# A hand-scheduled two-block network on one core: the order in which VectorE's tile transposes of the gated hidden layer are placed

## The reference

```python
def swiglu(x, w13, w2):                      # w13: 1024 x 5632, w2: 2816 x 1024
    a, b = jnp.split(x @ w13, 2, axis=-1)
    return (jax.nn.silu(a) * b) @ w2
...
for l in range(DEPTH):                       # first block
    x = layer_norm(ALPHA * x + 0.5 * swiglu(x, ffn1_w13[l], ffn1_w2[l]), ...)
    m = mixer(x, ...)
    x = layer_norm(ALPHA * x + m, ...)
    x = layer_norm(ALPHA * x + 0.5 * swiglu(x, ffn2_w13[l], ffn2_w2[l]), ...)
...
for layer in range(DEPTH):                   # second block
    h = swiglu_2(rms_norm(x, g[0]), ffn_w_in[layer, 0], ffn_w_out[layer, 0])
    x = x + 0.5 * rms_norm(h, g[1])
    h = token_mixer(rms_norm(x, g[2]), ...)
    x = x + rms_norm(h, g[3])
    h = swiglu_2(rms_norm(x, g[4]), ffn_w_in[layer, 1], ffn_w_out[layer, 1])
    x = x + 0.5 * rms_norm(h, g[5])
```

## Time and profile before

| what | value |
|---|---|
| median of three runs | 2129.59 us (2129.24 to 2132.51) |
| profiled execution, its own time | 2129.24 us |
| its span, first to last instruction | 2127.5 us |
| TensorE busy, matmuls | 2107.3 us, 99%, 10584 instructions |
| VectorE busy | 1698.3 us, 80%, 3204 instructions |
| ScalarE busy | 1075.8 us, 51%, 1540 instructions |
| mean granted TensorE clock | 0.999 |
| read from HBM | 390.75 MB, 184 GB/s |

### The profile page before, as it was taken

How to read it: one execution, slowest core, us unless ns; L and a number is a source line. 1 busy time by engine, 2 the same in 40 slices (tenths; PEclk the granted TensorE clock), 3 DMA queues, 4 the chain that set the end, 5 groups by cost and what they waited for, 6 DMA issues and landing times.

```text
span 2127.5 us, 28888 instructions
## 1 busy us (share of the span) xinstructions
PE 2107.3 (99%) x10584; PEld 1775.9 (83%) x10584; DVE 1698.3 (80%) x3204; ACT 1075.8 (51%) x1540; POOL 67.9 (3%) x107
## 2 busy tenths in 40 slices
PE   8999999999999999999999999999999999999998
PEld 7888999888888899978878888878888888888887
DVE  6887766888888867688888886789889888678886
ACT  5444553544444455444454446565445445665443
POOL 0000010000000001000010000010000000001000
PEclk9999999999999999999999999999999999999999
DMA  7766754666566574656656666337666665634663
GB/s 248 239 196 180 209 181 144 214 193 197 187 201 197 168 230 146 198 182 196 196 164 218 194 189 182 125 111 222 196 189 199 200 195 168 183 129 143 196 193 102
DMA packets 313952, 393.71 MB, mean 185 GB/s; under 512 B 17828, under 2 KB 272052, under 8 KB 313812
## 3 DMA queue, kind: packets, MB, share of 16 engines
q1 hardware_dynamic: 309120, 375.52, 57.7%
q0 software_dynamic: 4528, 16.29, 2.3%
q10 hardware_dynamic: 164, 0.06, 0.0%
HBM read 390.75 MB, written 1.05 MB: 184 GB/s over the span
## 4 chain that ended last, share of the span: by engine, by line
PE 90%; DVE 6%; DMA 2%; issue 1%; ACT 1%; SPq 0%; POOL 0%; DVEq 0%; POOLq 0%; ACTq 0%
PE bank L309 25%; PE bank L311 24%; PE bank L310 24%; PE bank L303 4%; PE bank L304 4%; PE bank L305 4%; DVE w_lo L293 2%; DVE hidden L464 1%; PE bank L1438 1%; PE bank L478 1%; PE bank L1459 1%; PE bank L972 1%; DMA stage<-in_mix_w_in 1%; DMA stage<-in_ffn_w_in 0%; DMA stage<-in_ffn_w 0%
## 5 line engine op out<-in xcount | busy, mean ns | idle before, releaser
L286 ACT ACTIVATE w_hi<-stage 128x1024 fp32r<-128x1024 f32 x711 | 746.1, 1058 | 649.9 <-PE bank L311 497.3
L293 DVE TENSOR_TENSOR w_lo<-stage,w_hi 128x1024 fp32r<-128x1024 f32 x711 | 864.9, 1224 | 228.3 <-ACT w_hi L286 221.4
L309 PE MATMUL bank<-w_hi,xt_hi 128*128 128x512 f32 x1760 | 691.9, 393 | 2.2 <-DVE w_lo L293 1.8
L311 PE MATMUL bank<-w_hi,xt_lo 128*128 128x512 f32 x1760 | 685.7, 390 | 0.0
L310 PE MATMUL bank<-w_lo,xt_hi 128*128 128x512 f32 x1760 | 685.6, 390 | 0.0
L464 DVE STREAM_TRANSPOSE hidden<-hidden 32x128 f32<-32x128 f32 (+1 forms) x1376 | 391.5, 285 | 21.4
L309 PEld LDWEIGHTS bank<-w_hi,xt_hi 128*128 128x128 f32 x1760 | 330.7, 188 | 73.6 <-issue 3.1
L311 PEld LDWEIGHTS bank<-w_hi,xt_lo 128*128 128x128 f32 x1760 | 330.6, 188 | 69.6
L310 PEld LDWEIGHTS bank<-w_lo,xt_hi 128*128 128x128 f32 x1760 | 330.9, 188 | 66.3
L309 PE MATMUL bank<-w_hi,mt_hi 128*128 128x512 f32 x768 | 303.3, 395 | 2.0 <-DVE mt_lo L546 2.0
L311 PE MATMUL bank<-w_hi,mt_lo 128*128 128x512 f32 x768 | 299.5, 390 | 0.0
(11 more groups left out here) (266 smaller groups left out, 1386.8 us busy)
## 6 DMA issues: line engine op xcount, KB each, us to landing
stage<-in_ffn_w SPq DMA_DIRECT2D x352, 256.0 KB, 3.2
stage<-in_ffn_w_in SPq DMA_DIRECT2D x352, 256.0 KB, 3.2
stage<-in_ffn_w SPq DMA_DIRECT2D x88, 512.0 KB, 3.7
stage<-in_ffn_w_out SPq DMA_DIRECT2D x88, 512.0 KB, 3.7
stage<-in_w_in SPq DMA_DIRECT2D x80, 512.0 KB, 4.2
stage<-in_mix_w_in SPq DMA_DIRECT2D x56, 512.0 KB, 4.1
stage<-in_w_out SPq DMA_DIRECT2D x16, 512.0 KB, 4.3
stage<-in_mix_w_out SPq DMA_DIRECT2D x16, 512.0 KB, 3.5
```

The costliest lines, as they stand in the source:

```text
L286: act.activation(w_hi[:, u % RING, :], stage[:, u % STAGED, :], ACT.Copy).then_inc(S["hi_ready"], 1)
L293: dve.tensor_tensor(w_lo[:, u % RING, :], stage[:, u % STAGED, :], f32(w_hi[:, u % RING, :]), ALU.subtract).then_inc(S["lo_ready"], 1)
L309: pe.matmul(o, m_hi, hi, start=first, stop=False)
L311: return pe.matmul(o, m_lo, hi, start=False, stop=last)
```

## The change

`pe_turns`: in stage 0 TensorE no longer turns (0,1) and (1,1), which VectorE's blocks take over. The tiles that TensorE turns in the other stages stay the same: (0,0), (0,10), (1,10); `turned_count` is written for the new list.

`block_turns` is no longer written by hand but worked out: the passes of a tile begin in the round after its last gu unit, and ht_hi and ht_lo follow when the rounds of its entry are over. Two tiles take four rounds, one takes two. What differs from the old table (begin, length, round of ht, tiles):

| stage | before | after |
|---|---|---|
| 0 | (0,1), (1,1) by TensorE | 8, 4, 12: (0,1), (1,1) |
| 0 | 16, 2, 18: (0,2) | 14, 2, 16: (0,2) |
| all others | 7, 1, 9: (0,1) and 10, 2, 12: (1,0) | 9, 4, 13: (0,1), (1,0) |
| all | 63, 2, 65: (1,9) | 62, 2, 64: (1,9) |

The entries with two tiles between them are the same (seven in stage 0, eight elsewhere).

ht_hi and ht_lo of (0,10) are still made in round 63, but no longer first in it: they stand in the common place, behind w_hi and w_lo of that round.

```diff
--- before.py
+++ after.py
@@ -428,11 +428,12 @@
 
         def pe_turns(s):
 
-            return [(0, 0)] + ([(1, 0), (0, 1), (1, 1)] if s == 0 else []) + [(0, STEPS - 1), (1, STEPS - 1)]
+            return ([(1, 0)] if s == 0 else []) + [(0, 0), (0, STEPS - 1), (1, STEPS - 1)]
 
         def turned_count(s, t, i):
-
-            return ffn_no(s) * 3 + (3 if s else 0) + pe_turns(s).index((t, i)) + 1
+            before = ffn_no(s) * 3 + (1 if s else 0)
+            order = [(0, 0)] + [e for e in pe_turns(s) if e != (0, 0)]
+            return before + order.index((t, i)) + 1
 
         def pe_turn_hidden(pe, s, t, v):
 
@@ -445,10 +446,13 @@
 
         def block_turns(s):
 
-
-            first = [(7, 1, 9, [(0, 1)]), (10, 2, 12, [(1, 0)])] if s else [(16, 2, 18, [(0, 2)])]
-            both = [(6 * i + 8, 4, 6 * i + 12, [(0, i + 1), (1, i)]) for i in range(1 if s else 2, STEPS - 2)]
-            return first + both + [(63, 2, 65, [(1, STEPS - 2)])]
+            begin = {}
+            for v in range(UNITS["ffn"]):
+                for i in range(STEPS):
+                    for t, u in ((0, v), (1, behind(s, v))):
+                        if u == gu_end(i) and (t, i) not in pe_turns(s):
+                            begin.setdefault(9 if s and t + i == 1 else v + 1, []).append((t, i))
+            return [(v, 2 * len(tiles), sorted(tiles)) for v, tiles in sorted(begin.items())]
 
         def blocks_count(s, n):
 
@@ -567,13 +571,11 @@
                 if s >= BLOCK2:
                     act_pre_sq(act, s, 1)
             for v in range(LAG if s else 0, n):
-                if v == turn_after(STEPS - 1) + 1:
-                    act_h(act, s, 0, STEPS - 1)
                 hi_upto(act, b + v + RING - LAG)
                 if s == 0 and v == TOGETHER + 3:
                     act_lower_bounds(act)
-                for g, (_, _, v1, tiles) in enumerate(block_turns(s)):
-                    if v == v1:
+                for g, (v0, length, tiles) in enumerate(block_turns(s)):
+                    if v == v0 + length:
                         for t, i in tiles:
                             act_h(act, s, t, i, g)
                 for i in range(STEPS):
@@ -581,7 +583,7 @@
                         act_silu(act, s, 0, i)
                     if behind(s, v) == gu_end(i):
                         act_silu(act, s, 1, i)
-                    if v == turn_after(i) + 1 and i < STEPS - 1 and (0, i) in pe_turns(s):
+                    if v == turn_after(i) + 1 and (0, i) in pe_turns(s):
                         act_h(act, s, 0, i)
                     if behind(s, v) == turn_after(i) + 1 and (1, i) in pe_turns(s):
                         act_h(act, s, 1, i)
@@ -626,15 +628,13 @@
                     dve_pre_var(dve, s, 1)
                 lo_upto(dve, b + 9)
             for v in range(LAG if s else 0, n):
-                if v == turn_after(STEPS - 1) + 1:
-                    dve_h(dve, s, 0, STEPS - 1)
                 lo_upto(dve, b + v + RING - LAG)
                 if s == 0 and v == TOGETHER + 2:
                     dve_tables(dve)
                 if s == 0 and v == TOGETHER + 4:
                     dve_lower_bounds(dve)
-                for _, _, v1, tiles in block_turns(s):
-                    if v == v1:
+                for v0, length, tiles in block_turns(s):
+                    if v == v0 + length:
                         for t, i in tiles:
                             dve_h(dve, s, t, i)
                 for i in range(STEPS):
@@ -642,11 +642,11 @@
                         dve_gate(dve, s, 0, i)
                     if behind(s, v) == gu_end(i):
                         dve_gate(dve, s, 1, i)
-                    if v == turn_after(i) + 1 and i < STEPS - 1 and (0, i) in pe_turns(s):
+                    if v == turn_after(i) + 1 and (0, i) in pe_turns(s):
                         dve_h(dve, s, 0, i)
                     if behind(s, v) == turn_after(i) + 1 and (1, i) in pe_turns(s):
                         dve_h(dve, s, 1, i)
-                for v0, length, _, tiles in block_turns(s):
+                for v0, length, tiles in block_turns(s):
                     if v0 <= v < v0 + length:
                         for a in range(4 * (v - v0) // length, 4 * (v - v0 + 1) // length):
                             dve_turn_blocks(dve, s, tiles, a)
```

## The result

The changed kernel takes 2151.58 us (median of four runs, 2150.47 to 2156.77) against 2131.05 us (2129.24 to 2132.93) for the kernel before, now with a fourth run: a ratio of 1.0101, 95% interval 1.0081 to 1.0121, so 1% slower. The profiled execution of it took 2148.35 us, 19.1 us more than the profiled one of before (2129.24). The direction was forecast; the 14.0 us were too few, and the median lies 1.6 us above the range.

A forecast was written before the change was run, and what follows sets the result against it. The prediction took TensorE, busy 99% of the span, to bound the kernel. Its terms, 7.7 - 3.5 + 9.8 = +14.0 us on 2129.24 us, gave 2143.2, or 2143.5 us as median; range 2134 to 2150 us.

The forecast's parts named there:

- Step 1: Round 63: h_lo(0,10), now behind eight blocks and lo(66), makes TensorE wait at round 64; +7.7 us.
- the bound of the step: Round 63: with only one of the two things ahead of h_lo(0,10), it would be in time; cost 0.
- Step 2: Ends of stages 0, 2, 3 and 5: earlier norm of tile 0 removes TensorE's two waits; -3.5 us.
- Step 3: Round 14: tiles (0,1) and (1,0), made later on VectorE, keep TensorE waiting; +9.8 us over the stages.
- its large terms: Round 14: later tiles cost +2.0 us in stage 0, and +2.2, +2.2, +2.6 us in stages 6, 8, 9.
- The small terms of stages 2, 3 and 11: Round 14: waits of 0.5 to 0.65 us with weights in time; net +0.35, +0.35, +0.6 us.
- stage 6's own terms: Round 14, stage 6: 1125.14 plus four w_lo (4.8) and three passes (3.8) put h_lo(0,1) at 1133.6; net +2.2 us.
- TensorE's clock falls in the long wait of stage 6: A 3.5 us idle stretch in stage 6 drops TensorE to 1.2 GHz; about 2150 us, chance 0.04.
- VectorE's relief decides: The 2.8 us of VectorE saved in each of seven stages removes TensorE's waits; 2122 us, chance 0.04.
- Slack takes it up: Late h tiles only replace TensorE's present waits; within 4 us of 2129.6 us, chance 0.08.
- Only one of the places costs: Either round 14 costs without round 63, or round 63 with small round 14 waits; 2134 to 2139 us, chance 0.2.

The follow-up runs named there:

- The two runs on round 63: Changed kernel with (0,10) first again in round 63: 2145.51 us; changed kernel with the blocks of (1,9) back in rounds 63 and 64: 2149.32 us.
- the idle holds: Kernel before, TensorE held idle at the start of round 30 of each of eight stages until h_lo(1,3) is made: 2170.59 us, ratio 1.0192.
- the one entry alone: Kernel before with (0,1) and (1,0) together in rounds 9 to 12, ht in 13, in stages after the first: 2144.78 us, ratio 1.0066.
- the filled holds: Kernel before, TensorE held at round 30 of eight stages until h_lo(1,3) is made, working through 14 extra matmuls each time: 2158.48 us, ratio 1.0131.

## Why the prediction failed

**Step 1 held in mechanism and size.** 7.7 us forecast, 8.0 measured: the first matmuls of round 64 are 7.4 us late in all, and the sum had left out the 0.08 us or so that each of them takes longer behind its wait. The two runs on round 63 show that each of the two things ahead of h_lo(0,10) is nearly free alone, as the bound of the step had it.

**Step 2 held, and was sized too low.** -3.5 against -4.7 us. The two waits of a stage, shown as 0.48 and 0.23 us idle, cost TensorE 0.70 and 0.46 us, 1.16 together, where the step had 0.87. That the early norm is the cause is shown by the run that has the early blocks alone: 4.6 us faster than before.

**Step 3 held at its large terms.** In stage 0 TensorE's restart was put at 46.85 and came at 46.88; stages 6, 8 and 9 together were put at +7.0 and gave +6.9, though not each (2.2, 2.2, 2.6 against 1.7, 1.9, 3.3), since they follow the landing of unit 12. That the three add up to what was forecast is in part luck. The small terms of stages 2, 3 and 11 were sized at half, 2.6 us against 1.3: TensorE was 0.8 to 1.0 us late there and not 0.5 to 0.65. Two readings in the working are off without effect: w_hi of unit 66 is there at 1081.2 and not 1081.0, and stage 6's own terms add up to 1133.7 and not 1133.6.

Without the clock the terms measured give 8.0 - 4.7 + 2.2 + 2.6 - 0.6 + 6.9 = 14.4 us, where 14.0 was forecast.

**The step that failed is the sum's silence on the clock.** The prediction had it as a rival, "TensorE's clock falls in the long wait of stage 6", with a chance of 0.04 and about 2150 us (5 us for the clock), and left the term out of the sum and the range's upper end. It happened in the first profile, in stage 0 and stage 9, for 4.5 us, in the second in stages 6 and 9, and in the idle holds in seven of eight. Had the term been in, 2143.5 + 4.5 = 2148.0 would have met the profiled execution (2148.35), and a range moved up with it the median. The reason for the 0.04 was that the longest idle time in the work, 1.76 us, had left no mark in the trace of before; but between its first matmuls and its last that trace holds no longer wait, so it was no evidence for waits of 2 to 3.5 us.

The prediction also says that nothing in the trace of before shows idleness bringing the half rate back. Both its ends do. At the start TensorE is idle until 5.18, and for 1.09 us more before 7.36; the matmuls behind that start 0.43 us apart, as they do at 0.50 in the changed kernel (the granted clock reads 1.00 there, but no record of it stands before 10.76), and from 12.04 on 0.23 us apart. And TensorE's last matmul ends at 2121.02, after which the clock falls (windows of TensorE with the columns used above):

```profile
8.94 0.63 PE L310 MATMUL bank<-w_lo,xt_hi 128*128 128x512 f32 x1
9.37 0.63 PE L311 MATMUL bank<-w_hi,xt_lo 128*128 128x512 f32 x1
...
12.04 0.40 PE L310 MATMUL bank<-w_lo,xt_hi 128*128 128x512 f32 x1
12.28 0.39 PE L311 MATMUL bank<-w_hi,xt_lo 128*128 128x512 f32 x1
```

```profile
2120.00:2123.00 3.00, 1.02 (x5) 1.00 0.00 0
2123.00:2124.00 1.00, 0.00 (x0) 0.80 0.00 0
2124.00:2127.50 3.50, 0.00 (x0) 0.50 0.40 150
```

A clock of 0.80 over the middle microsecond puts the fall at 2123.6, so 2.6 us of idle time had been enough once; the slices of 53 us hide it. The Trainium skill (TensorE: Matmul & The Clock Gate, Part 1) speaks of the half rate as the state an idle TensorE returns to, and the runs agree: 0.50 behind idle waits, 1.00 when the same time is filled.

**The medians.** The profiled execution is the fastest of five of the changed kernel; the median is 3.2 us above it. The second profile's execution (2150.94 us, 2.6 us above the first) has 1.9 us more of waits for h_lo, from later landings, and half-clock stretches of its own, which cost 4.2 us where the first had 4.5. For the slowest run (2156.77 us) no profile exists, but its mean granted clock is on record: 0.995, where the other four of the five have 0.997. By 0.002 of 2155 us that would be 4.3 us, an estimate with some 2 us either way from the rounding, of the 5.2 us by which it is above the median. The rest stays open.

**The rivals.** "VectorE's relief decides" is refuted by the one entry alone (1.0066). "Slack takes it up" is refuted by the table: the steps stay in the difference to the end. "Only one of the places costs" is refuted, since both did.

## What to carry to other kernels

When one engine is busy 99% of the span, ask of each reordered helper instruction what stands ahead of it on its own engine at its due time; two neighbours that are each free can be late together. Work with which the helper fills its dead time before a late landing costs nothing there; moved behind the landing it is in the way (here TensorE was 1.7 to 3.3 us later in each of stages 6, 8 and 9). A forecast of new TensorE waits of some 2.5 us or more needs a term for the clock behind them (in stage 9 it was 2.8 us behind a wait of 3.2 us); if such a wait can't be avoided, matmuls into a free bank kept the clock up in both kernels that had them. And the start and the end of a trace, where TensorE is idle, are worth a window of their own: they showed here what idle time does to the clock before any wait was added.

## What the runs showed of the hardware

The clock after a wait isn't the same from one execution to the next: 2.52 us of idle time in stage 0 was followed by half clock in one profile of the changed kernel and not in the other. Inside the work, idle waits of 3.2 us and more were followed by it in 15 of 16 cases in the profiles above, those of 2.38 to 2.84 us in 3 of 10. In the profile of the filled holds, which had none of the long idle waits, it came once behind 1.82 us of idle time in stage 5. The other waits of under 2 us left it at 1.00, one of 1.87 us in the changed kernel's second profile too.
